# The feed-forward stage of an encoder layer as seven half-size products per product

## What is computed

```python
z = rmsnorm(h, norm1_g) @ w_in                     # 1024 -> 1792
mix = groups of (short convolution | pooling | Fourier) of z, each normed
h = h + mix @ w_out                                # 1024 -> 1024
v = rmsnorm(h, norm2_g)
gate, up = split(v @ w_gate_up)                    # 1024 -> 2 x 2816
h = h + (silu(gate) * up) @ w_down                 # 2816 -> 1024
return rmsnorm(h, final_g)                         # without the 16 first tokens
```

## Time and profile before

| | us |
|---|---|
| median of 3 runs | 2714.98 (2713.02 to 2715.85) |
| span of the profiled execution, first to last instruction | 2716.6 |
| PE busy in it | 2617.7, 96% |
| DVE, ACT, POOL busy | 1085.4, 786.7, 163.8 |
| share of TensorE's full clock, mean | 0.980 |
| moved by DMA | 273.41 MB, 101 GB/s |

### The profile page before, as it was taken

The page is one execution under the profiler, slowest core; times in us unless marked ns, Lnnn a source line. Parts: engine busy times, 40 slices in busy tenths (PEclk is TensorE's granted clock), DMA queues, the critical chain, the costliest instruction groups (busy, mean ns, idle before and its releaser), DMA issues.

```text
span 2716.6 us, 32424 instructions
## 1 busy us (share of the span) xinstructions
PE 2617.7 (96%) x11852; PEld 2166.0 (80%) x11852; DVE 1085.4 (40%) x1366; ACT 786.7 (29%) x1055; POOL 163.8 (6%) x206
## 2 busy tenths in 40 slices
PE   7999999789999999999999999999999999999998
PEld 5888887777888887888887788888788888788886
DVE  4544455546333236333326333324533324533322
ACT  4111110333333223333223333222333322322211
POOL 0000000030000011000011000011000011000000
PEclk9999999779999999999999999999999999999999
DMA  5011101552333333333334333334233344233331
GB/s 183 20 58 58 54 27 41 164 190 78 100 93 93 123 102 140 95 99 100 109 109 140 101 93 100 106 115 159 78 95 98 99 119 154 92 94 100 93 95 61
DMA packets 89573, 273.41 MB, mean 101 GB/s; under 512 B 12580, under 2 KB 20038, under 8 KB 89505
## 3 DMA queue, kind: packets, MB, share of 16 engines
q1 hardware_dynamic: 88897, 270.47, 31.4%
q0 software_dynamic: 608, 1.93, 0.2%
HBM read 248.70 MB, written 23.67 MB: 100 GB/s over the span
## 4 chain that ended last, share of the span: by engine, by line
PE 75%; DVE 1%; ACT 1%; issue 1%; DMA 0%; POOL 0%; SPq 0%; DVEq 0%; POOLq 0%; ACTq 0%
PE fin_bank L68 25%; PE fin_bank L70 25%; PE fin_bank L69 25%; PE fin_bank L1423 1%; DVE v_lo_sb L1327 1%; ACT v_hi_sb L1250 0%; DMA w_raw_sb<-w_panels 0%; DVE stage_sb L1341 0%; ACT mix_raw_sb L1244 0%; DVE h_sb L1309 0%; DVE h_sb L1392 0%; DVE w_panel_lo_sb L719 0%; DVE stage_sb L1320 0%; ACT w_panel_hi_sb L714 0%; POOLq L1117 0%
## 5 line engine op out<-in xcount | busy, mean ns | idle before, releaser
L719 DVE TENSOR_TENSOR w_panel_lo_sb<-w_raw_sb,w_panel_hi_sb 128x1024 fp32r<-128x1024 f32 x370 | 452.3, 1225 | 1055.3 <-ACT w_panel_hi_sb L714 1055.3
L68 PE MATMUL fin_bank<-v_hi_sb,w_panel_hi_sb 128*128 128x512 f32 x1760 | 690.2, 392 | 13.9 <-DVE v_lo_sb L1327 13.9
L69 PE MATMUL fin_bank<-v_lo_sb,w_panel_hi_sb 128*128 128x512 f32 x1760 | 688.8, 391 | 0.0
L70 PE MATMUL fin_bank<-v_hi_sb,w_panel_lo_sb 128*128 128x512 f32 x1760 | 688.6, 391 | 0.0
L714 ACT ACTIVATE w_panel_hi_sb<-w_raw_sb 128x1024 fp32r<-128x1024 f32 x370 | 390.1, 1058 | 914.9 <-PE fin_bank L70 895.5
L68 PEld LDWEIGHTS fin_bank<-v_hi_sb,w_panel_hi_sb 128*128 128x128 f32 x1760 | 333.1, 189 | 84.0 <-issue 15.0
L70 PEld LDWEIGHTS fin_bank<-v_hi_sb,w_panel_lo_sb 128*128 128x128 f32 x1760 | 332.9, 189 | 70.2
L69 PEld LDWEIGHTS fin_bank<-v_lo_sb,w_panel_hi_sb 128*128 128x128 f32 x1760 | 333.2, 189 | 69.4
L68 PE MATMUL fin_bank<-w_panel_hi_sb,act_hi_sb 128*128 128x512 f32 x880 | 348.0, 396 | 0.0
L69 PE MATMUL fin_bank<-w_panel_lo_sb,act_hi_sb 128*128 128x512 f32 x880 | 348.0, 396 | 0.0
L70 PE MATMUL fin_bank<-w_panel_hi_sb,act_lo_sb 128*128 128x512 f32 x880 | 348.0, 395 | 0.0
(11 more groups left out here) (150 smaller groups left out, 2245.0 us busy)
## 6 DMA issues: line engine op xcount, KB each, us to landing
w_raw_sb<-w_panels SPq DMA_DIRECT2D x370, 512.0 KB, 3.6
x_tiles_sb<-x SPq DMA_DIRECT2D x20, 512.0 KB, 5.6
h_sb<-x SPq DMA_DIRECT2D x20, 512.0 KB, 7.0
out<-stage_sb SPq DMA_DIRECT2D x20, 512.0 KB, 4.0
mix_raw_sb<-mixT SPq DMA_DIRECT2D x34, 256.0 KB, 3.0
table_raw_sb<-table SPq DMA_DIRECT2D x24, 344.0 KB, 3.3
mixT<-mix_tiles_sb SPq DMA_DIRECT2D x24, 256.0 KB, 2.1
xf<-xf_stage_sb SPq DMA_DIRECT2D x20, 128.0 KB, 1.7
```

Source lines behind the costliest of these rows:

```text
L68: pe.matmul(out, w[0], x[0], start=first, stop=False, skip_group_check=True)
L69: pe.matmul(out, w[0], x[1], start=False, stop=False, skip_group_check=True)
L70: return pe.matmul(out, w[1], x[0], start=False, stop=last, skip_group_check=True)
L719: dve.tensor_tensor(self.w_lo[:, s, :], self.w_raw[:, s, :], self.w_hi[:, s, :].bitcast(F32), ALU.subtract)\
```

## The change

`finish` is gone. In its place stand three functions, each a block of its own, which go through DRAM in between:

- `outproj`: the out projection for all five blocks. It holds h and the raw mix tiles twice and transposes the normed v of block b-1 after k = 2 of block b. It writes h to DRAM (`h1`) and the transposed v too (`vT`).
- `gateup`: the product v @ w_gate_up by seven products of half size. The contraction (1024) is cut into halves of 512 (4 tiles), the columns into the gate half and the up half, the tokens into pairs of runs (two of 428, or two of 424; three such sequences k). The seven sums of v (`v_form`) are made once for each k on DVE; the products land in three banks for each of two column tiles (a, b, c of y = 0, 1), and DVE and ACT recover the four results from these. A unit is one 128x512 piece of weight: 12 matmuls of 428 or 424 columns, stationary weight. 33 iterations have 14 units each. DVE then makes the seven sums of the activation, and POOL stores them (`act_forms`).
- `down`: seven products again: 77 units for each of three groups of 4, 3 and 3 pairs of token tiles. A unit is 3 matmuls of 512 columns for each pair, and loads one weight piece and one piece of activation. DVE adds each finished product into h once to four times (`UPDATES`, 14 adds for a pair over the seven forms).

The sums of the weights that the seven products need are made by DMAs in DRAM, issued by POOL (`Forms`): eight waves, four of copies and four of accumulating DMAs. Those for gate and up (5.77 MB a wave, in four pieces of 176 rows of 8 KB) are issued between the `rms` steps of `project`; those for down (2.88 MB a wave) in iterations 1 to 8 of `gateup`. The loops on all engines are now written out, so the program is longer: 10043 rows on PE where there were 2955.

```diff
+HALVES = (428, 428, 424)
+SEQ_AT = (0, 428, 856)
+TOKEN_AT = (1704, 848, 0)
...
+    def copy(self, pool, w, piece, t, src):
+        pool.dma_start(self.sums(t)[piece], src[piece], max_dma_last_dim=8192).then_inc(self.made[w % 2], 16)
+    def add(self, pool, w, piece, t, src):
+        pool.dma_start(self.sums(t)[piece], src[piece], accum_op=ALU.add, max_dma_last_dim=8192)\
+            .then_inc(self.made[w % 2], 16)
...
+    def wave(self, pool, w, piece):
+        T1, T3, T2, T4, q = self.T1, self.T3, self.T2, self.T4, self.quadrant
+        if w == 0:
+            self.copy(pool, w, piece, T1, q(self.B12))
+        elif w == 1:
...
+        elif w == 2:
+            self.wait(pool, 0)
+            self.add(pool, w, piece, T1, q(self.B11))
...
+        elif w == 4:
+            self.wait(pool, 2)
+            self.copy(pool, w, piece, T2, self.sums(T1))
+        elif w == 5:
+            self.wait(pool, 4)
+            self.add(pool, w, piece, T2, q(self.B22))
+        elif w == 6:
+            self.wait(pool, 5)
+            self.copy(pool, w, piece, T4, self.sums(T2))
+        else:
+            self.wait(pool, 6)
+            self.add(pool, w, piece, T4, q(self.B21))
...
-            with pool.Fori(1, NBLK + 1) as r:
+            for r in range(1, NBLK + 1):
                 for t in range(NT):
                     rms(tile(r, t), P, t)
+                    if r >= 2:
+                        n = NT * (r - 2) + t
+                        for piece in (2 * (n % 2), 2 * (n % 2) + 1):
+                            gu.wave(pool, n // 2, piece)
...
+            def vt_store(b):
+                sp.wait_ge(vt_made, 8 * b + 8)
+                sp.dma_start(c["vT"][:, token(b):token(b) + T].rearrange("(k p) n -> p k n", p=P), vt[:, :, :])\
+                    .then_inc(vt_stored, 16)
...
                     ins.then_inc(w_used, 1)
+                    if b and k == LAST[0]:
+                        transposes(b - 1, 24 * b)
...
+            transposes(NBLK - 1, 24 * (NBLK - 1) + 16)
...
+def gateup(nc, c, gu, dn, w_landed):
...
+    ACC = (a_of, b_of, c_of, b_of, a_of, c_of, b_of)
...
+            def v_load(k):
+                if k:
+                    sp.wait_ge(v_lo_made, FORMS * k)
+                t0, n = TOKEN_AT[k], HALVES[k]
+                for slot, row, at in ((A11, 0, t0), (A21, 0, t0 + n), (A22, 512, t0 + n), (A12, 512, t0)):
+                    sp.dma_start(vraw[:, slot, :, 0:n],
+                                 c["vT"][row:row + 512, at:at + n].rearrange("(k p) n -> p k n", p=P))\
+                        .then_inc(v_landed, 16)
...
+            for i in range(ITER):
+                k, m = divmod(i, HF)
+                n, at = HALVES[k], SEQ_AT[k]
+                pool.wait_ge(a_summed, 4 * i + 4)
+                for f, src in ((0, left[:, 0, :]), (1, asum[:, 1, :]), (2, right[:, 0, :]), (3, asum[:, 0, :]),
+                               (4, left[:, 1, :]), (5, asum[:, 2, :]), (6, right[:, 1, :])):
+                    pool.dma_start(c["act_forms"][f, m, :, at:at + n], src[:, 0:n]).then_inc(a_stored, 16)
+                if 1 <= i <= 8:
+                    for piece in range(dn.pieces):
+                        dn.wave(pool, i - 1, piece)
+            pool.wait_ge(a_stored, 16 * FORMS * ITER)
...
+            def v_step(k, f):
+                v_split(k, f)
+                if f == 0:
+                    v_sum(k, D_)
+                    v_sum(k, N6)
+                    v_sum(k, E_)
+                elif f == 1:
+                    v_sum(k, S3)
...
+            def read_out(u):
+                i, f, y = place(u)
+                n, now = HALVES[i // HF], 2 * i + y + 1
+                acc = bank[:, ACC[f](y), 0:n]
+                if f == 1:
+                    dve.wait_ge(used, u + 1)
+                    dve.wait_ge(s1_made, now)
+                    dve.tensor_tensor(u2[:, y, 0:n], acc, s1[:, y, 0:n], ALU.subtract).then_inc(u2_made, 1)
+                elif f == 3:
+                    dve.wait_ge(used, u + 1)
+                    dve.tensor_tensor(u3[:, y, 0:n], acc, s1[:, y, 0:n], ALU.subtract).then_inc(u3_made, 1)
+                    dve.wait_ge(u3_made, now)
+                    dve.tensor_tensor(u3[:, y, 0:n], bank[:, c_of(y), 0:n], u3[:, y, 0:n], ALU.add).then_inc(c22_made, 1)
+                elif f == 5:
+                    dve.wait_ge(used, u + 1)
+                    dve.tensor_tensor(u2[:, y, 0:n], acc, u2[:, y, 0:n], ALU.add).then_inc(c12_made, 1)
+                    dve.wait_ge(c12_made, now)
+                    dve.wait_ge(sl_made, now)
+                    dve.wait_ge(a_stored, 16 * FORMS * i)
+                    dve.tensor_tensor(left[:, y, 0:n], u2[:, y, 0:n], sl[:, y, 0:n], ALU.mult).then_inc(left_made, 1)
+                elif f == 6:
...
+                if f == 0 and i:
+                    pe.wait_ge(sl_made, now - 2)
+                elif f == 1 and i:
+                    pe.wait_ge(c21_made, now - 2)
+                elif f == 2 and i:
+                    pe.wait_ge(c12_made, now - 2)
+                elif f == 3:
+                    pe.wait_ge(u2_made, now)
+                elif f == 4:
+                    pe.wait_ge(s1_made, now)
+                elif f == 5:
+                    pe.wait_ge(c22_made, now)
+                elif f == 6:
+                    pe.wait_ge(u3_made, now)
+                s = u % SLOTS
+                for k in range(4):
...
+def down(nc, c, dn, landed, half, eps):
...
+            dn.all_made(sp)
+            for u in range(ALL):
+                k, v = divmod(u, UNITS)
+                first, n = PAIRS[k]
+                f, j = divmod(v, HF)
+                if u >= SLOTS:
+                    sp.wait_ge(w_lo_made, (u - SLOTS) // 2 + 1)
+                sp.dma_start(w_raw[:, u % SLOTS, :], weights(u)).then_inc(landed[u % SLOTS], 16)
+                if u >= SLOTS:
+                    sp.wait_ge(a_lo_made, u - SLOTS + 1)
+                sp.dma_start(a_raw[:, u % SLOTS, 0:P * n], c["act_forms"][f, j, :, P * first:P * (first + n)])\
+                    .then_inc(landed[u % SLOTS], 16)
...
+            def update(k, f, i):
+                g = FORMS * k + f
+                dve.wait_ge(used, UNITS * k + HF * (f + 1))
+                if f == 0:
+                    dve.wait_ge(h_landed[k % 2], pieces_landed(k))
+                else:
+                    dve.wait_ge(acc_read, reads_before(g))
+                for r, c_half, op in UPDATES[f]:
+                    part = h[:, k % 2, r, i, UNIT * c_half:UNIT * c_half + UNIT]
...
+                for i in range(PAIRS[k][1]):
+                    ins = split_product(pe, bank[:, 4 * (g % 2) + i, :], [x[:, s, P * i:P * i + P] for x in (a_hi, a_lo)],
+                                        [w[:, s, :] for w in (w_hi, w_lo)], j == 0, j == HF - 1)
+                ins.then_inc(used, 1)
```

943 lines of the change are left out of this document (627 added, 316 removed).

## The result

| | before | after |
|---|---|---|
| median, us | 2715.32 | 2561.85 |
| runs, us | 2713.02 to 2715.85 | 2558.72 to 2564.68 |
| span of the profiled execution | 2716.6 | 2563.1 |

The ratio is 0.943, with an interval of 0.9415 to 0.9445: 5.7% less time. One run of each, in this series or a later one, lay thousands of us above its fellows and is left out (10926.79 after, 4394.57 before). The forecast was 2543, the range 2515 to 2620; measured were 19 us more than forecast.

A forecast was written before the change was run, and what follows sets the result against it. PE, busy 96% of the span, was taken as the bound. Matmuls -215.3, gaps +39.8 and waves +3 sum to -172.5 us: span 2716.6 becomes 2544.1, median 2543 us, range 2515 to 2620.

The forecast's parts named there:

- starved in down: Rival: small pieces arrive too slowly in down; 30 us, 2573; chance 0.17 shared with gate/up waiting for read-outs.
- the read-outs of gate/up: Rival: PE waits 1.5 us for read-outs in each of 33 iterations; 50 us, 2593; chance 0.17 shared with starved down.
- slow chain: Rival: adding waves, one behind another, hold up `project`; from 52 GB/s downward slower than before, 2818 at 40; chance 0.05.
- Gate/up's matmuls, 1058.7: Gate/up: 3696 matmuls of 428 columns at 0.1915 us and 1848 of 424 at 0.1899, 1058.7 us in all.
- the straight line between 344 and 512 columns: Gate/up's matmul price, interpolated between 0.156 us at 344 columns and 0.2267 at 512: 0.1915 for 428, 0.1899 for 424.
- Down's matmuls, 538.9: Down: 2310 matmuls of 512 columns at 0.2333 us, 538.9 us in all.
- transposes 3.7: Out projection: 32 transposes of the block before cost 3.7 us of gap in each of four more blocks.
- 2 to 3 us a block: Out projection: extra cost if k = 0 to 2 no longer cover the square, root and norm.
- The gap to gate/up, 46.5: From the last projection matmul into gate/up: norm, transposes, v's store and load, splits, sums, slow first iteration; 46.5 us.
- The gap to down: Between gate/up and down: last sums, their stores and landing, barrier, first pieces, splits, slow clock; 26 us.
- The waves, 3: The DMA waves that form weight sums, mostly hidden, add 3 us by meeting other transfers; nothing to 12 possible.
- The adds' price: In the waves, an accumulating DMA was priced at twice a copy: 32 us a wave against 16, 180 GB/s.

The follow-up runs named there:

- experiment 1: Kernels with TensorE's split-product matmuls alone, the whole layer left out, at widths from 344 to 512 columns: 428 columns take 0.195 us, 512 columns 0.2266.
- experiment 5: The changed kernel with one transpose of the four for each bank in the out projection: 2562.27 us, ratio 0.944.
- experiment 4: The changed kernel without the eight waves of copies and accumulating DMAs for either set of sums, quadrants read in place of sums: 2553.42 us, ratio 0.9407.

## Why the prediction was right

It named the mechanism: PE's time in matmuls fell, gaps grew, the waves stayed nearly hidden. Its sum was near in part by luck (below). Its rivals did not come: PE isn't starved in down (264 GB/s at full PE), the read-outs of gate/up hold PE for 7.8 us in all, and the adds are no slow chain. Point by point, with the 19 us that it was off:

- **Gate/up's matmuls, 1058.7: mis-sized by 14.9.** 22 iterations of 32.6 us and 11 of 32.4 are 1073.6. The step that failed is the straight line between 344 and 512 columns. It has two points and no width between, and the price bulges above it (experiment 1). The forecast named 0.2267 as the other end of the price, but its range has no term for any price above the line.
- **Down's matmuls, 538.9: measured 523.7** (2310 x 0.2267). Shape and operands were those of the earlier trace rows, yet the price was the old down's own. The out projection before had 0.2267 too, at the same shape, which I didn't look up; its term, 224.0, is 217.6, but on both sides of the change, so that the saving doesn't feel it. The other two missed by +14.9 and -15.2, errors of different origin that cancelled by luck: with the measured prices the matmuls are 2030.5 us before and 1814.9 after, 215.6 less, where 215.3 were forecast.
- **What is left of the 19 us is in the gaps.** They were 95.2 us before (88.8 by the forecast, which priced the old out projection too high) and are 150.8: 55.6 more, where 39.8 were forecast. The other 3.5 lie ahead of the out projection.
- **The blocks of the out projection.** Without the matmuls I had 44 us, measured are 60.6. Two terms make this. First, "transposes 3.7": it priced PE's work, and in the last block, where nothing holds them, 32 transposes do take 3.4. In three blocks of four DVE's reading of eight banks sets them, 1.7 us of wait and 5.0 to 5.6 for the 32 (experiment 5): 9.6 us more than forecast in all. The forecast gave the lost cover "2 to 3 us a block" and left it out of the sum. Second, the clock: the block's window has 0.94 for a granted clock, a mean of the levels 1.2 and 2.4 GHz, and behind the statistics, in which PE moves one column a matmul, some products come 0.43 us apart: 14 in the first block, then 7, 8, 5 and 12, which costs 3.3 us and then 1.5 to 2.9 a block. I had counted them for the first block alone; the others make 7.8. The statistics themselves took 2.6 to 3.0 in place of 3.6, 3.3 less.
- **The gap to gate/up, 46.5** with 8 us for norm and transposes and 6 for the first iteration: without these 32.5, measured 29.5, and each link was near (store and barrier 7.3 for 10, load 11.5 for 12, DVE's split and sums 7.7 for 7.8). First iteration 37.1 against 32.6: 4.5 for 6. The changes of sequence: 34.8, 33.8, 34.6 and 33.6 in four iterations, 6.6 us over the undisturbed, for 5.
- **The gap to down**: 24.5 for 23.7. Refill and slow start 9.3 us in down for 5.3: one wait of 4.8 us in down's first units. Tail 14.9 for 12: the last h is read in pieces as before.
- **The waves, 3**: the start of `outproj` came 6.5 us later than `finish` did, of which experiment 4 gives some 5.3 to the waves in `project`. The adds' price was right: 11.5 MB of waves 2 and 3 hold the engines from 165 us until about the end of ACT's wait at 227.65, 184 GB/s, for 180. What I had not placed is who suffers: not POOL, but the small store that ACT waits for: the kind of the earlier trace rows, a round later, where the kernel before waited 3.05 us and the changed one 8.70.
- On the rule of two reads for an add, in the Trainium skill ("Collectives: The Full Stack", section "The bandwidth ceiling: the fold count and why AG ≠ RS ≠ AR"): the trace has a factor of 1.7 for its half (213 against 363 GB/s at 99% busy), and not a rate of 32 GB/s.

## What to carry to other kernels

Price a matmul by a row of its own width; where there is none, keep both ends, and look whether the same shape has another price elsewhere in the trace. When work is halved that writes into banks another engine must empty, price the emptying. A wait at a stage's head has several ends: before moving one load ahead, follow the second and third product too, for PE only exchanges an early stop for a later one.
